# Expert stage of a mixed GLA, mixture-of-experts and delta-rule model: fp32 products in three fp32r passes, weight splitting on three engines

## What is computed

```python
def hier_moe(h, w_rg, w_re, w_e_in, w_e_out):
    ...
    gates = jnp.einsum('tk,tke->et', weights, jax.nn.one_hot(eid, N_EXPERTS, dtype=jnp.float32))

    def body(acc, inp):
        wi, wo, ge = inp
        a, u = jnp.split(t @ wi, 2, axis=-1)
        return acc + ((jax.nn.silu(a) * u) @ wo) * ge[:, None], None

    y, _ = lax.scan(body, jnp.zeros(t.shape, jnp.float32), (w_e_in, w_e_out, gates))
```

## Time and profile before

| | before |
|---|---|
| median of 3 runs | 2873.13 us (2872.28 to 2873.95) |
| the profiled execution, its own time | 2872.07 us |
| its span, first to last instruction | 2870.3 us |
| mean granted PE clock over the span | 0.921 of full |
| expert loop, first up product to last down product | 570.2 to 987.8 us |
| one pair of tiles in the steady part | 26.25 us |

### The profile page before, as it was taken

The page is one execution under the profiler, slowest core; times in us unless marked ns, Lnnn a source line. Parts: engine busy times, 40 slices in busy tenths (PEclk is TensorE's granted clock), DMA queues, the critical chain, the costliest instruction groups (busy, mean ns, idle before and its releaser), DMA issues. The chain is left out here.

```text
span 2870.3 us, 26011 instructions
## 1 busy us (share of the span) xinstructions
PE 2394.8 (83%) x9359; PEld 1588.0 (55%) x9359; DVE 1128.1 (39%) x1481; ACT 729.0 (25%) x1031; POOL 188.1 (7%) x231
## 2 busy tenths in 40 slices
PE   5899776398889658996788849999979955899999
PEld 1442465244444323443777726888857733688887
DVE  1003653211111142566555454433356844444433
ACT  1113222012221112232222203222224255332222
POOL 0000000100000100000222101000000011010000
PEclk8999988599999978998888979999989978999999
DMA  6025216388888501221000002323212200223221
GB/s 266 30 66 190 75 65 253 118 302 318 322 324 317 212 25 52 73 73 37 1 0 0 1 29 88 98 94 101 96 51 82 80 0 0 67 95 102 95 96 59
DMA packets 68288, 312.16 MB, mean 109 GB/s; under 512 B 7236, under 2 KB 8448, under 8 KB 59904
## 3 DMA queue, kind: packets, MB, share of 16 engines
q1 hardware_dynamic: 50832, 250.17, 25.2%
q0 software_dynamic: 10256, 37.83, 3.3%
q10 hardware_dynamic: 7136, 23.30, 2.0%
HBM read 273.50 MB, written 37.77 MB: 108 GB/s over the span
## 5 line engine op out<-in xcount | busy, mean ns | idle before, releaser
L777 PE MATMUL ps<-ff_hhi,ff_whi 128*128 128x512 f32 x704 | 276.7, 393 | 8.6 <-DVE ff_hlo L1911 8.3
L778 PE MATMUL ps<-ff_hhi,ff_wlo 128*128 128x512 f32 x704 | 275.3, 391 | 0.0
L779 PE MATMUL ps<-ff_hlo,ff_whi 128*128 128x512 f32 x704 | 275.2, 391 | 0.0
L212 PE MATMUL ps<-hn,ring 128*128 128x512 f32 x608 | 265.0, 597 | 0.7 <-PEq L1258 0.7
L1829 DVE TENSOR_TENSOR ff_wlo<-ring,ff_whi 128x1024 fp32r<-128x1024 f32 x132 | 163.6, 1239 | 247.3 <-ACT ff_whi L1825 247.3
L1135 PE MATMUL ps<-w_up,hgT 128*128 128x512 f32 x512 | 225.1, 598 | 24.5 <-ACT hgT L1168 24.5
L1825 ACT ACTIVATE ff_whi<-ring 128x1024 fp32r<-128x1024 f32 x132 | 139.3, 1055 | 406.8 <-PE ps L779 299.8
L212 PEld LDWEIGHTS ps<-hn,ring 128*128 128x128 f32 x608 | 116.5, 192 | 147.4 <-issue 147.4
L1135 PEld LDWEIGHTS ps<-w_up,hgT 128*128 128x128 f32 x512 | 96.5, 191 | 143.6 <-issue 115.5
L777 PEld LDWEIGHTS ps<-ff_hhi,ff_whi 128*128 128x128 f32 x704 | 133.1, 189 | 38.9 <-DVE ff_wlo L1829 10.6
L778 PEld LDWEIGHTS ps<-ff_hhi,ff_wlo 128*128 128x128 f32 x704 | 133.0, 189 | 27.8 <-issue 0.5
(11 more groups left out here) (439 smaller groups left out, 3826.9 us busy)
## 6 DMA issues: line engine op xcount, KB each, us to landing
ring<-stream SPq DMA_DIRECT2D x276, 512.0 KB, 3.5
w_up<-experts SPq DMA_DIRECT2D x32, 2048.0 KB, 8.0
w_down<-experts SPq DMA_DIRECT2D x32, 1024.0 KB, 9.8
y_dram<-zeros POOLq DMA_DIRECT2D x1, 16384.0 KB, 54.9
y_dram<-ytile ACTq DMA_DIRECT2D x32, 512.0 KB, 10.7
tab<-table ACTq DMA_DIRECT2D x1, 2586.0 KB
res<-xT ACTq DMA_DIRECT2D x1, 2048.0 KB, 27.8
h_dram<-mix SPq DMA_DIRECT2D x4, 512.0 KB, 2.8
```

The costliest lines, as they stand in the source:

```text
L212: m = pe.matmul(out, w[:, k * P:(k + 1) * P], act[:, k, :], start=k == 0, stop=k == KT - 1)
L777: pe.matmul(out, w_hi, a_hi, start=start, stop=False)
L778: pe.matmul(out, w_lo, a_hi, start=False, stop=False)
L779: return pe.matmul(out, w_hi, a_lo, start=False, stop=stop)
```

## The change

Every product of the expert loop becomes three fp32r passes. The weights of a pair are 12 blocks of 128x1024 (8 of up, 4 of down). ACT rounds a block to one of four buffers `w_hi`; the rest is written over the raw weights, by DVE for nine blocks and by POOL for blocks 2, 6 and 10 of each pair. ACT may round block n+4 when PE has used block n. Tokens and hidden tiles are rounded on ACT and their rest is taken on DVE. The tiles of the next pair are turned inside this pair's products: tile 0 ahead of block 6, tile 1 after block 9.

```diff
-                    for u in range(2):
-                        pool.wait_ge(M["turned"][u], i + 1)
-                        apart(pool)
-                        pool.tensor_copy(idx[:, u, :], tok_i[:, bass.ds(i * 2 + u, 1)]).then_inc(M["idx_set"][u], 1)
...
+                    pool.wait_ge(idx_set, i + 1)
+                    for u in range(2):
+                        gather(u, idx[:, u:u + 1])
+                    rest_of_block(i, 6)
+                    rest_of_block(i, 10)
+                    for u in range(2):
+                        pool.wait_ge(M["y_a"][u], i + 2)
+                        pool.wait_ge(M["y_b"][u], i + 2)
+                        pool.wait_ge(M["put_set"][u], i + 1)
+                        put(u, ytile[:, u, :], idx[:, 2 + u:3 + u])
+                        if u == 0:
+                            rest_of_block(i, NB + 2)
```

```diff
+                        for b in range(4):
+                            up(i, u, b)
+                            if (u, b) == (1, 1):
+                                pe.wait_ge(M["gathered"][0], i * 16 + 32)
+                                pe.wait_ge(M["copied_hi"][1], i + 1)
+                                pe.wait_ge(M["copied_lo"][1], i + 1)
+                                turn_tokens(0)
+                            if (u, b) == (1, 2):
+                                turn_hidden(i, 0)
...
+                    down(i, 0, 0)
+                    turn_hidden(i, 1)
+                    down(i, 0, 1)
+                    pe.wait_ge(M["gathered"][1], i * 16 + 32)
...
+                    turn_tokens(1)
...
+                    for f in range(2):
+                        down(i, 1, f)
```

`block` numbers in `up` and `down` are n = 4u + b and n = 8 + 2u + f; each does two columns of 512 in three passes, then raises `w_used`. The functions new to the loop on POOL are these:

```diff
+                def gather(u, at):
+                    pool.sem_inc(gathering, 1)
+                    pool.indirect_dma_start(
+                        out=hg[:, u, :], out_offset=None, in_=h2_dram,
+                        in_offset=bass.IndirectOffsetOnAxis(ap=at, axis=0),
+                        bounds_check=T - 1, oob_is_err=False).then_inc(M["gathered"][u], 16)
+
+                def put(u, rows, at):
+                    pool.sem_inc(gathering, 1)
+                    pool.indirect_dma_start(
+                        out=y_dram, out_offset=bass.IndirectOffsetOnAxis(ap=at, axis=0), in_=rows, in_offset=None,
+                        bounds_check=2 * T - 1, oob_is_err=False).then_inc(M["y_stored"][u], 16)
```

Empty slots now carry the number 4096, which lies outside both tables, so their rows are neither gathered nor stored. A result row goes to the place of its token in `y_dram` (1024 rows instead of 5120), so the way back is four plain loads on SP, and `clear_results` with its empty block is gone:

```diff
-        fast_project_out("mixout", mix, STREAM["out"].start, lambda n: mod[:, 16 + n, 0:1], STREAM["gdn"].start + SLOTS,
-                    clear_results)
+        fast_project_out("mixout", mix, STREAM["out"].start, lambda n: mod[:, 16 + n, 0:1], STREAM["gdn"].start + SLOTS)
...
-            @block.gpsimd
-            def _(pool):
...
+            @block.sync
+            def _(sp):
                 for t in range(TT):
-                    for a in range(2):
-                        pool.indirect_dma_start(
...
+                    sp.dma_start(yrow[:, :, t, :], y_dram.rearrange("(a t p) d -> t p a d", a=2, p=P)[t]
+                                 ).then_inc(rows_back[t], 16)
```

More of the change, by code:

```diff
@@ L39 @@
 MAXTILES = 40
-MINTILES = 2 * T // P
+NO_TOKEN = 4096.0
 class Cols:
@@ L126, in program, with over @@
     with ExitStack() as ctx:
+        home = {}
         def sb(name, shape, dt=F32, on=None):
-            return (on or ctx).enter_context(nc.sbuf_tensor(name, shape, dt))
+            made = (on or ctx).enter_context(nc.sbuf_tensor(name, shape, dt))
+            home[name] = nc.sbuf_base - 4 * int(np.prod(shape[1:]))
+            return made
+        def over(name, shape, dt, below, skip=0):
+            return nc.alloc_sbuf_tensor_at(name, shape, dt, offset=home[below] + skip)
         live = []
@@ L1082, in program, with raw_block @@
-        dma_names = ("up_in", "down_in", "gathered", "y_stored")
+        credited = ("hid_hi", "hid_lo", "y_a", "y_b")
+        gathering, hg_set, idx_set = sem("gathering"), sem("hg_set"), sem("idx_set")
+        w_rounded, w_split_ve, w_split_pool, w_used = (
+            sem(n) for n in ("m_w_rounded", "m_w_split_ve", "m_w_split_pool", "m_w_used"))
+        NB = 12
+        ON_POOL = (2, 6, 10)
+        ON_VE = tuple(n for n in range(NB) if n not in ON_POOL)
+        def raw_block(n, up, down):
+            n = n % NB
+            if n < 8:
+                return up[:, n // 4, (n % 4) * 1024:(n % 4 + 1) * 1024]
+            return down[:, (n - 8) // 2, (n % 2) * D:(n % 2 + 1) * D]
@@ new lines, in _ @@
+                pool.wait_ge(hg_set, 2)
+                turns = pairs(pool)
+                def gather(u, at):
[9 more added lines that the diff above has]
+                        bounds_check=2 * T - 1, oob_is_err=False).then_inc(M["y_stored"][u], 16)
@@ L1103, in _, with rest_of_block @@
+                def rest_of_block(i, n):
+                    pool.wait_ge(w_rounded, i * NB + n + 1)
+                    pool.tensor_tensor(raw_block(n, w_up_lo, w_down_lo), raw_block(n, w_up, w_down),
+                                       w_hi[:, n % 4, :].bitcast(F32), ALU.subtract).then_inc(w_split_pool, 1)
+                for u in range(2):
+                    put(u, hg[:, u, :], nowhere[:, :])
                 pool.wait_ge(h_stored, TT * 16)
-                turns = pairs(pool)
+                for u in range(2):
+                    pool.wait_ge(M["y_stored"][u], 16)
+                    gather(u, moves[:, 0, u:u + 1])
@@ new lines, in split_here, with up @@
+                def split_here(i, n):
+                    if n in ON_VE:
+                        pe.wait_ge(w_split_ve, i * len(ON_VE) + ON_VE.index(n) + 1)
+                    else:
+                        pe.wait_ge(w_split_pool, i * len(ON_POOL) + ON_POOL.index(n) + 1)
+                def up(i, u, b):
+                    n = 4 * u + b
+                    split_here(i, n)
+                    for kk in range(2):
+                        k, c = 2 * b + kk, slice(kk * 512, (kk + 1) * 512)
+                        m = three(pe, ps[:, 4 + u, :], hgT_hi[:, u, k, :], hgT_lo[:, u, k, :],
+                                  w_hi[:, n % 4, c], raw_block(n, w_up_lo, w_down_lo)[:, c],
+                                  k == 0, k == KT - 1)
+                    m.then_inc(w_used, 1)
@@ new lines, in round_block, with tokens_hi @@
+                def round_block(n):
+                    act.activation(w_hi[:, n % 4, :], raw_block(n, w_up, w_down), ACT.Copy).then_inc(w_rounded, 1)
+                def tokens_hi(u, pair):
+                    act.wait_ge(M["turned"][u], pair + 1)
+                    act.activation(hgT_hi[:, u, :, :].rearrange("p k n -> p (k n)"), flat(ps[:, 6:8, :]), ACT.Copy
+                                   ).then_inc(M["copied_hi"][u], 1)
+                act.wait_ge(M["up_in"][0], 16)
+                for n in range(4):
+                    round_block(n)
```

271 lines of the change are left out of this document (165 added, 106 removed).

## The result

The changed kernel takes 2921.01 us (2919.23 to 2923.03), the kernel before beside it 2873.54. The ratio is 1.0163, with a 95% interval from 1.015 to 1.0176. The profiled execution has a span of 2917.4 us against 2870.3, 47.1 us more.

What follows compares the result with a forecast made beforehand. PE was taken to bound the loop, 417.6 us for 16 pairs. The loop's -15, the zeros' -9 and the edges' -1.3 made -25 on the profiled 2872.07, so 2847, median 2848 us, range 2790 to 2890.

Steps and rivals of the forecast that it cites:

- The chain: In the loop, from T, the end of a turn's last block: rest, result, put, index copy, then gather at T+7.8.
- The first pair: First pair of the loop: next gathers issued early, no store ahead; 23 us with the slow clock at its start.
- The way back from the landing: In the loop, from the gathered tile's arrival through transposes and blocks 6 to 11: 4.1 and 7.8 us, 11.9 in all.
- The zeros: Before norm n2: without their DMA 5.7 us go, 2.3 of clock and about 1 of barrier, -9 us; at worst 0.
- The DMA engines: In the loop: 6.8 MB a pair take 19 us, which fits under the forecast pairs, so DMA is not the bound.
- rival (a): In the loop: gathers aren't held, start at T+5.3, no gap reaches the clock; pair 21.7, kernel 2793 us; chance 0.18 with between.
- the landing: In the loop, the gather of tile 0 from issue to arrival: 4.5 us, with ends of 3.3 and 9.3.
- The term that was too small: the clock: In the loop, PE's slower clock after a 3.5 us gap: 0 to 2.3 us a pair, taken as 1.1.
- rival (b): In the loop: the landing replaces PE's time once landing and clock exceed 7.3 us; kernel up to 2938 us; chance 0.26.
- Edges: Before the loop -1 us (-3 to +5), behind it -1 (-4 to +3); with routing's +0.7, together -1.3.
- The collision on the port: At the pair's turn: POOL's rest holds the shared port until T+2.7, so DVE's rest of block 3 ends at T+3.9.
- The case against a held DMA issue: On POOL: the skill page restricts the lock to GpSimd operations reading SBUF; by that rule the sum is 11 us lower.

Runs made afterwards that it cites:

- e5: Changed kernel with six unused fp32 products keeping PE at work while it waits for the gather: 2899.0 us, ratio to before 1.0091.
- e3: Changed kernel with the 16.8 MB of zeros written again, into a tensor nothing reads, and waited for: 2926.9 us, ratio to before 1.0185.
- e4: Changed kernel with the first 2 MB load of up weights held until the gathered tile 0 is being turned: 2888.3 us, ratio to before 1.0046.
- e6: Changed kernel with the first two gathers issued ahead of the two empty puts: 2917.7 us, ratio to before 1.0151.
- e9: Changed kernel with the edits of e1, e6 and e2 together: 2786.0 us, ratio to before 0.9691.
- e8: Changed kernel with the edits of e1 and e6 together: 2812.6 us, ratio to before 0.9787.
- e2: Changed kernel with all twelve rests of the weight blocks on DVE and none on POOL: 2900.0 us, ratio to before 1.0088.
- e1: Changed kernel with the gathers issued a pair earlier, each ahead of the put of the same tile: 2815.3 us, ratio to before 0.9792.

## Why the prediction was wrong

It forecast 2848 us with a range to 2890; 2921 lies outside. Step by step:

**What held.** The chain was the right one, within 0.3 us where it rests on the order of work. The gather was forecast for T+7.8 and came at T+8.07; DVE's rest of block 3 ended at T+4.2 (T+3.9), its result at T+4.9 (T+4.8). POOL's rest of 1024 columns was estimated at 2.4 us and took 2.40. The first pair took about 22.5 us (23). The way back from the landing at full clock takes 12.0 us, as e5 shows (11.9). The zeros gave 7.6 us with the routing's steps (8.3 forecast), and e3 ties it to them, with 5.9 at the end, and to their landing, which is what the prediction assumed. The DMA engines let the pair through (0.57 of the time). One reading was off without weight in the sum: under rival (a) DVE and POOL are said to have 4 us of room each, but by the prediction's own 17, 11 and 18.7 us it is DVE that has 4.7, POOL 10.7 and ACT 3.0.

**The term that failed: the landing.** It was put at 4.5 us and is 7.2 (7.5 in the mean of tile 0). That is 2.7 us a pair, 40 us over 15 pairs. The choice between 4.5 and 9.3 was made by the number of rows and the absent stores: "A quarter of the rows, with no stores of whole tiles beside them, is nearest to the lower rows". The run e4 shows what a landing hangs on here instead, namely what is in flight when the gather is issued: 3.6 us without the weight load, 7.2 with it. The number of rows was no bad guide by itself: without the load they land in less than 4.5 us. That the load would be there could be read from the order: it is released when block 3 is done, T+5.4 by the prediction's 1.36 us a block (T+6.4 measured), and the gather stands at T+7.8. The prediction names it under rival (b), "`w_up` is being loaded just then", but counts it as one argument among others and not as a term. The lower rows, the gathers back, came from behind the loop (995 to 1005 us), where they were all that the DMA queues moved.

**The term that was too small: the clock.** The prediction put the price between 0 and 2.3 and took 1.1, since the gap of 3.5 us lay at the edge. The gap became 6.15 us, and e5 puts the price at 2.0 in the pair shown and 1.8 in the mean. This is 0.7 to 0.9 us a pair, 10 to 13 us. It is only in part a consequence of the landing: with one of 3.6 us (e4) the gap was 2.5 to 2.9 us in most pairs, and yet the clock fell behind 13 of 14 landings.

Put into the prediction's own sum: 8.07 + 7.2 + 11.9 + 2.0 = 29.2, against 29.36 measured over the four pairs up to 716 us, and 15 x 29.36 + 22.5 = 462.9 for the loop, measured 462.75. So it was rival (b) that described the case. Its own formula at 7.2 us gives a pair of 29.2, a loop of 461 and a kernel of 2906; most of the 15 us that are still missing are the edges. Its chance of 0.26 was too low, and the part of it left outside the range was the part that happened.

**Edges.** Forecast -1 and -1, measured +5.7 and +4.0. At the start POOL stands idle for 8.1 us until an empty put has landed. With the order turned (e6) this stretch is 4.9 us shorter, and the kernel 3.3. Behind the loop POOL's last put starts 5.5 us after the last product, since both engines still make rests for a pair that doesn't exist; it lands in 2.6 us (DMA to landing of that one put, from 1036.61), and SyncE's loads start at 1045.35. With the rests off POOL the stretch is 27.6 us instead of 29.3 (e9, the last product's end at 899.0 to the transposes at 926.59). Before, it was 25.3. The other 2.3 are not explained.

**The collision on the port.** The prediction had this mechanism from two rows of another stage and placed it rightly on the chain: DVE's rest at the pair's turn takes 2.89 us. What it left out is the cost to DVE's other rests, which shows once the gather is off the chain: e8 to e9 is 26.6 us. The Trainium skill, SBUF — State Buffer, section SBUF: two separate sides, gives the reason, a port that one of the two engines holds for a whole instruction. The trace agrees: 2.89 us is what remains of POOL's 2.40 us operation from 709.52, 1.80 us, and DVE's own 1.1 to 1.2. The case against a held DMA issue fared worse: in e2, where POOL makes no elementwise operation but an index copy, the issue of the second gather takes 1.93 us in each pair beside DVE's rests, and 1.00 in the first turn, where no rest runs. But the first gather takes 1.13 and the puts 0.98 to 1.03 beside rests too, so what decides it is open.

## What to carry to other kernels

A transfer on the chain that ends last was priced here by what else was in flight when it was issued (3.6 us or 7.2). So look up which queue starts what in the microseconds ahead of it, and take its time from rows with the same neighbour. Prefetch a small transfer by a whole turn rather than by the shortest time that seems to do: here the place of two DMA issues in one queue was worth 106 us, and turned 47 us lost into 58 won. Work that was handed from VectorE to GpSimd in the form of operations with two SBUF inputs was no relief; compare the time of VectorE's own operations before and after. And look at more than one pair before calling a clock kept: in e4 the pair shown first is the exception.

## What the runs showed of the hardware

- A gather of 128 row slots lands in 3.6 us with no load issued just ahead (e4), in 7.2 us with a 2 MB load issued 1.7 us ahead, in 9.3 us in e1, and in 10.9 and 12.7 us among the first 6 MB of weights (e6).
- Slots outside the bounds still cost packets: from 600 to 950 us the changed kernel's 48 gathers and puts have 6912 packets, 144 each, though a tile has 32 tokens on average. Under 512 B it has 13892 packets, the kernel before 7236. The second of the two empty puts, which store nothing, landed after 11.3 us beside the first weights.
- PE left idle for 6.15 us resumed at a granted clock of 0.50 for 5.2 us; kept at work with useless products it stayed at 0.99. After 2.50 us of idle time and another 1.02 it went on at 1.00 in one pair of e4, after 2.54 us and another 0.98 it fell to 0.50 in the next. In an earlier pair the eight transposes behind 2.92 us of idle time took 1.97 us, the low clock at once (at 632.48).
- The issue of a gather on GpSimd took 1.00 us when VectorE did nothing with two SBUF inputs, and 1.13 to 1.94 beside VectorE's rests (e2); the issue of a put stayed at 0.98 to 1.03 there. A one-column index copy on GpSimd takes 1.2 us in e1 (median of 32), against 0.18 in the kernel before and 0.14 for VectorE's own.
